# Two merge stages of a one-core hybrid layer: seven block products in place of eight, with sums by accumulating transfers and on VectorE

## The reference

```python
o_a = attend(q_a, k_all, v_all) @ w_pa
...
o_g = rms_norm(o_g, g_gla).reshape(B, T, GLA_V) * jax.nn.silu(r_g)
o_g = o_g @ w_pg
g_a, g_b = jnp.split(jax.nn.sigmoid(gates), 2, axis=-1)
mix = (g_a * o_a + g_b * o_g) @ w_out
```

## Time and profile before

| | us |
|---|---|
| median of 3 runs | 2679.12 (2678.48 to 2681.05) |
| the profiled execution | 2678.96 |
| its span | 2677.1 |
| TensorE busy | 2538.2 (95%) |
| VectorE busy | 1662.4 (62%) |
| ScalarE busy | 1329.9 (50%) |
| GpSimd busy | 285.5 (11%) |

### The profile page before, as it was taken

How to read it: one execution, slowest core, us unless ns; L and a number is a source line. 1 busy time by engine, 2 the same in 40 slices (tenths; PEclk the granted TensorE clock), 3 DMA queues, 4 the chain that set the end, 5 groups by cost and what they waited for, 6 DMA issues and landing times.

```text
span 2677.1 us, 37871 instructions
## 1 busy us (share of the span) xinstructions
PE 2538.2 (95%) x15199; PEld 1938.3 (72%) x15199; DVE 1662.4 (62%) x2553; ACT 1329.9 (50%) x2262; POOL 285.5 (11%) x287
## 2 busy tenths in 40 slices
PE   7999699999999999999999999996899999999994
PEld 3574499999788587676767888883677777777773
DVE  2654678886333435757576434656777767777775
ACT  3542467776423324444344332442666767666663
POOL 1441101000000001010101000000010101111012
PEclk9999899999999999999999999997899999999997
DMA  9320000000211100101012201535698888989886
GB/s 332 129 90 8 0 1 1 1 1 1 73 38 71 62 16 20 36 18 38 7 34 83 79 32 37 192 118 211 229 313 308 273 315 288 313 282 310 304 273 215
DMA packets 176608, 345.06 MB, mean 129 GB/s; under 512 B 9338, under 2 KB 37580, under 8 KB 176434
## 3 DMA queue, kind: packets, MB, share of 16 engines
q1 hardware_dynamic: 166396, 314.09, 32.9%
q0 software_dynamic: 9472, 28.32, 4.1%
q10 hardware_dynamic: 566, 0.24, 0.0%
HBM read 304.35 MB, written 38.27 MB: 128 GB/s over the span
## 4 chain that ended last, share of the span: by engine, by line
PE 63%; issue 22%; DMA 8%; DVE 4%; ACT 2%; POOL 1%; SPq 0%; POOLq 0%; DVEq 0%; ACTq 0%
PE ps L1100 16%; PE ps L1449 7%; PE ps L851 6%; DMA ffn_scratch<-WK 6%; PE ps L823 5%; PE ps L1409 5%; PE ps L228 4%; PE ps L1991 4%; PE ps L1512 2%; PE ps L1495 1%; PE ps L1423 1%; PE ps L2556 1%; PE ps L2017 1%; PE ps L1472 1%; PE ps L1393 1%
## 5 line engine op out<-in xcount | busy, mean ns | idle before, releaser
L2617 ACT ACTIVATE RWr<-R 128x1024 fp32r<-128x1024 f32 x384 | 377.8, 1054 | 73.6 <-PE ps L2556 69.9
L2712 DVE TENSOR_TENSOR W_low<-R,RWr 128x1024 fp32r<-128x1024 f32 x256 | 301.5, 1221 | 77.3 <-ACT RWr L2617 75.2
L2556 PE MATMUL ps<-RWr,R1r 128*128 128x512 f32 x1024 | 329.6, 396 | 6.0 <-DVE R1r L2700 4.2
L1100 PE MATMUL ps<-W_high,tile_high 128*128 128x512 f32 x640 | 250.9, 392 | 7.8 <-DVE W_low L1178 7.3
L1100 PE MATMUL ps<-W_low,tile_high 128*128 128x512 f32 x640 | 250.4, 391 | 0.0
L1100 PE MATMUL ps<-W_high,tile_low 128*128 128x512 f32 x640 | 250.4, 391 | 0.0
L2556 PEld LDWEIGHTS ps<-RWr,R1r 128*128 128x128 f32 x1024 | 193.0, 188 | 58.2 <-issue 14.2
L1170 DVE TENSOR_TENSOR tile_low<-R,tile_high 128x1024 fp32r<-128x1024 f32 x80 | 97.9, 1224 | 156.8 <-ACT tile_high L1126 156.6
L1449 PE MATMUL ps<-R3r 128*128 128x512 f32 (+1 forms) x640 | 188.5, 371 | 2.9 <-issue 2.9
L2712 DVE TENSOR_TENSOR tile_high<-R,RWr 128x1024 fp32r<-128x1024 f32 x128 | 150.9, 1220 | 29.9 <-ACT RWr L2617 29.6
L2556 PE MATMUL ps<-RWr,R3r 128*128 128x512 f32 x512 | 167.7, 399 | 0.0
(11 more groups left out here) (373 smaller groups left out, 5069.8 us busy)
## 6 DMA issues: line engine op xcount, KB each, us to landing
R<-in_w_dram SPq DMA_DIRECT2D x96, 2048.0 KB, 13.3
RW<-in_w_in_dram SPq DMA_DIRECT2D x11, 1024.0 KB, 5.3
R<-in_w_mod_dram SPq DMA_DIRECT2D x5, 2048.0 KB, 14.0
RW<-in_w_in_dram SPq DMA_DIRECT2D x5, 2048.0 KB, 7.8
RW<-in_w_mod_dram SPq DMA_DIRECT2D x4, 2048.0 KB, 12.1
WK<-in_w_mod_dram SPq DMA_DIRECT2D x3, 2048.0 KB, 7.7
mix_scratch<-R SPq DMA_DIRECT2D x10, 512.0 KB, 2.6
R<-mix_scratch SPq DMA_DIRECT2D x10, 512.0 KB, 6.1
```

The lines of the kernel that those rows point to most:

```text
L1100: i = pe.matmul(bank(m % 4), Tsplit[a][:, m % 2, k, :], Wsplit[b][:, k, :], start=(k == 0 and n == 0), stop=(k == KD - 1 and n == 2))
L2556: m = pe.matmul(bank(bank_of(e, i, j)), stat[a][:, k, :], w[b][:, k % 2, :], start=(k == 0 and z == 0), stop=(k == KD - 1 and z == 2))
L2617: act.activation(ring_high[n % RING], pair_raw[i][j][:, 2 * q:2 * q + 2, :], ACT.Copy).then_inc(S("weights_high"), 1)
L2712: dve.tensor_tensor(ring_low[n % RING], pair_raw[i][j][:, 2 * q:2 * q + 2, :], ring_high[n % RING].bitcast(F32), ALU.subtract).then_inc(S( ...
```

## The change

Each product of (1280 x 1024) by (1024 x 1024) is now cut into blocks and done with seven block products in place of eight. Tiles are taken in five pairs p (tiles 2p and 2p+1 are the two block rows), the inner dimension in two halves of four chunks, the weight matrix in four blocks of 512 rows by 512 columns. A step is now one combination c of seven for one pair: 4 chunks by 3 matmuls, 12 in all, and there are 7 x 5 x 2 = 70 steps in a merge (two halves g of 35 steps; g is one whole product). Merge A does o_a first (g = 0) and its gates second (g = 1); merge B does its gates first.

- Rows: three of the seven combinations take raw rows; the others take sums S1, S2, S4, S3, which DVE makes in place (`rows_sum`, L1342 to L1350), 4 per pair, 40 per merge, 512 columns each. In the second half of merge A they go into the output blocks, since h is still needed.
- Weights: blocks are summed in place by 1 MB accumulating transfers from SBUF to SBUF that POOL issues (L1404), 4 per half, 8 per merge, each behind the one before it. Seven combinations by 4 chunks are split per half: 56 chunks per merge where 32 were.
- Outputs: c = 0 goes to a bank, ACT copies it out (`move`), c = 1 accumulates on the same bank and gives block 11. The others are summed by DVE into the output blocks (`block_sum`, L1329 to L1333), 60 per merge; c = 5 accumulates on the bank of c = 4 after DVE has read that bank. Six banks in a ring.
- Gates and products: sigmoid on ACT after the last sum of a block, then the product on DVE (`product`, L1365), 20 per merge. In merge A the product follows one or two steps behind the sum.
- Tiles are split three steps ahead, into four half-size buffers.
- Merge A's mix is stored when its rows are done, for odd tiles after c = 6, the last combination. Merge B no longer loads it: POOL adds it from `mix_scratch` at the end by ten accumulating transfers of 512 KB (L1416), and the output stage's first two turns wait for them.
- PE also waits for `state_moved` before merge B.

```diff
+        def staggered(x, y):
+            return [(x, 0), (x, 1), (y, 0), (x, 2), (y, 1), (x, 3), (y, 2), (x, 4), (y, 3), (y, 4)]
+        ORDER = staggered(0, 1) + [(c, p) for p in range(PAIRS) for c in (2, 3)] + staggered(4, 5) + [(6, p) for p in range(PAIRS)]
+        W_BLOCK = {0: (0, 0), 1: (1, 0), 2: (0, 0), 3: (1, 1), 4: (1, 1), 5: (0, 1), 6: (1, 0)}
+        ROW_SUM_OF = {2: "S1", 3: "S4", 4: "S2", 5: "S3"}
+        W_SUM_OF = {2: 1, 5: 2, 4: 3, 6: 4}
+        AHEAD = 3
+        BANKS = 6
+            w_split_at[-1 if C < 1 else 0 if C < 2 else last_step[C - 2] + (3 if C == COMBOS else 0)].append(C)
...
-                        for n, (a, b) in enumerate(((high, high), (high, low), (low, high))):
-                            i = pe.matmul(bank(m % 4), Tsplit[a][:, m % 2, k, :], Wsplit[b][:, k, :], start=(k == 0 and n == 0), stop=(k == KD - 1 and n == 2))
+                    if c == 1:
+                        pe.wait_ge(S("gates_made"), made["move", g, p])
+                    elif c == 5:
+                        pe.wait_ge(S("tiles_merged"), merged["sum", g, p, "12", 4])
+                    elif q >= BANKS:
+                        bank_read(pe, q - BANKS)
...
+                        if name == "S2":
+                            i = dve.tensor_tensor(S2, a11, S1, ALU.subtract)
+                        elif name == "S4":
+                            i = dve.tensor_tensor(S4, a12, S2, ALU.subtract)
+                        else:
+                            i = dve.tensor_tensor(S2, a22, S2, ALU.subtract)
...
+                    for nth, (dst, src, c) in enumerate(((r11, r12, 0), (r12, r22, 0), (r22, r11, 3), (r21, r22, 1))):
+                        pool.wait_ge(S("weights_split"), split + HALF_K * (c + 1))
+                        weights_landed(pool, g, nth)
+                        pool.dma_start(dst, src, accum_op=ALU.add).then_inc(S("tiles_in2"), 16)
...
+                            pool.wait_ge(S("tiles_merged"), merged["product", 1, p, "12" if i == 0 else "21"])
+                            pool.dma_start(mix[:, t, :], mix_dram[t * P:(t + 1) * P, :], accum_op=ALU.add).then_inc(S(f"tiles_in{i}"), 16)
...
-            for t in range(NT):
-                if t in (0, KD):
-                    sp.wait_ge(S("tile_out") if t == 0 else S("gated_out_turned"), GH * NI if t == 0 else GH * NT)
-                sp.dma_start(mix[:, t, :], mix_dram[t * P:(t + 1) * P, :]).then_inc(S("R3_moved"), 16)
...
+                if t < 2:
+                    pe.wait_ge(S(f"tiles_in{t}"), 16 * (len(range(t, NT, 3)) + PAIRS))
```

More of the change, by code:

```diff
@@ new lines, in dve_after @@
+        def dve_after(tag, m):
+            ops = []
+            for back, when in ((2, {4: ("12",), 5: ("22",), 6: ("21",)}), (1, {1: ("11",)})):
+                if 0 <= m - back < MS and (tag, steps_m[m - back][0]) == (0, 1):
+                    g, c, p = steps_m[m - back]
+                    ops += [("product", g, p, b) for b in when.get(c, ())]
+            if m + AHEAD < MS and steps_m[m + AHEAD][1] == 4:
+                g, c, p = steps_m[m + AHEAD]
+                ops.append(("rows", g, p, "S3"))
+            if m < MS:
+                g, c, p = steps_m[m]
+                for b in {2: ("22",), 3: ("12",), 4: ("12",), 5: ("22", "21"), 6: ("21",)}.get(c, ()):
+                    ops.append(("sum", g, p, b, c))
+                    if (tag, g) == (1, 1) and c >= 4 and (b, c) != ("21", 5):
+                        ops.append(("product", g, p, b))
+                if c == 1 and (tag, g) == (1, 1):
+                    ops.append(("product", g, p, "11"))
+            if 0 <= m - 1 < MS and steps_m[m - 1][1] == 1:
+                g, c, p = steps_m[m - 1]
+                ops += [("rows", g, p, name) for name in ("S1", "S2", "S4")]
+            return ops
@@ new lines, in counted @@
+        def counted(tag, after, base):
+            table = {}
+            for m in range(MS + 2):
+                for op in after(tag, m):
+                    table[op] = base + len(table) + 1
+            return table
+        act_done, dve_done, bases = [], [], (0, 0)
+        for tag in range(2):
+            act_done.append(counted(tag, act_after, bases[0]))
+            dve_done.append(counted(tag, dve_after, bases[1]))
+            bases = (bases[0] + len(act_done[tag]), bases[1] + len(dve_done[tag]))
@@ new lines, in act_merge @@
+                for m in range(MS + 2):
+                    if m + AHEAD < MS:
+                        tile_high(m + AHEAD)
+                    for C in w_split_at.get(m, ()):
+                        weights_high(C)
+                    ops = act_after(tag, m)
+                    for name, *at in ops:
+                        if name == "gate" and at[2] != "11":
+                            gate(*at)
+                    if m < MS and steps_m[m][1] < 2:
+                        act.wait_ge(S("merge_tile_done"), m0 + m + 1)
+                    for name, *at in ops:
+                        if name == "move":
+                            move(*at)
+                        elif at[2] == "11":
+                            gate(*at)
@@ new lines, in dve_merge @@
+                tile_low(0)
+                for C in w_split_at[-1]:
+                    weights_low(C)
+                tile_low(1)
+                for m in range(MS + 2):
+                    if m in behind:
+                        behind[m](dve, ch)
+                    if m == 0:
+                        for n in range(2, AHEAD):
+                            tile_low(n)
+                    if m + AHEAD < MS:
+                        tile_low(m + AHEAD)
+                    for C in w_split_at.get(m, ()):
+                        weights_low(C)
+                    for name, *at in dve_after(tag, m):
+                        if name == "rows":
+                            rows_sum(*at)
+                        elif name == "sum":
+                            dve.wait_ge(S("merge_tile_done"), m0 + m + 1)
+                            block_sum(*at)
+                        else:
+                            if at[2] == "11" and tag == 1:
+                                dve.wait_ge(S("merge_tile_done"), m0 + m + 1)
+                            product(*at)
```

351 lines of the change are left out of this document (222 added, 129 removed).

## The result

The changed kernel takes **2631.93 us** (median of four runs, 2627.85 to 2633.42) against 2680.09 us of the kernel before on the same chip: a ratio of 0.982, 95% interval 0.980 to 0.983, or 48 us less. The forecast was 2630 us, within 2620 to 2652. Two more rounds of the same kernel on other occasions gave 2634.05 and 2635.20 us (ratios 0.982 and 0.983); single runs of it lie between 2626 and 2636 us.

The account below looks back on a forecast made before the run. The prediction took the merges to be bound by the number of matmuls. Merge A's terms sum to -24.3 us and merge B's to -24.5, together -48.8 from 2678.96 us: 2630 us, range 2620 to 2652.

Parts of the forecast that it names:

- 120 matmuls fewer, each merge: Both merges: 960 matmuls become 840, all on the path at 0.2267 us each, 27.2 us less per merge.
- waits for VectorE, each merge: TensorE stalls 2.3 us beside steps 53 to 64 of the second half, 0.2 us in the first: 2.5 us.
- half-clock beginning, against before: Start of each merge: matmuls at half clock after TensorE stood still, said to come back whatever is done later.
- end of merge A: Between merge A's last matmul and GLA's first: block sum, sigmoid and product follow one another, 1.4 us more.
- start of merge B: First steps of merge B: two half-size steps ready before VectorE finishes GLA's last tiles, gain 0.3 us.
- weight sums: POOL's 1 MB transfers in both merges: cost 0 at 11.5 us each, costing from 15.3 us on.
- end of merge B, to the second turn of mix: After merge B: the last addition of mix lands between hidden and 1.3 us late, taken as 0.5 us.
- the rival of 2650 us: Both merges: each of 140 step starts costs TensorE a hand-over of 0.14 us, 19.6 us; chance 0.10.
- no stall: Both merges: VectorE's lag never reaches TensorE, so stalls vanish, 2625 us or 2623 us; chance 0.15.
- VectorE bound: Stretches of c = 4 and 5 in both merges: VectorE's slower instructions bound them, 2643 us; chance 0.17.
- the 17 pairs: Steps 53 to 64: 17 of 53 VectorE instructions directly behind what they read, each 0.12 us more.
- the rival that ended slower: Weight sums land late, costing 12L - 201 us at L us per transfer, 2729 us at 25; chance 0.07 beyond break-even.

Follow-up runs that it names:

- e7: Changed kernel with the block sum first in c = 4 steps and 18 and 28 identity products ahead of merges A and B: 2629.58 us, ratio 0.9815.
- e1: Changed kernel with VectorE's block sum put ahead of tile split and weight chunks in c = 4 steps: 2631.66 us, ratio 0.9815.
- e2: Changed kernel with twelve more VectorE subtractions of 512 columns in each merge's second half, beside steps 53 to 64: 2646.6 us, ratio 0.9875.
- e6: Changed kernel with 18 and 28 unused identity products on TensorE ahead of merges A and B: 2632.75 us, ratio 0.982.
- e8: Changed kernel with the block sum first in c = 4 steps and 8 and 11 identity products ahead of merges A and B: 2627.0 us, ratio 0.9795.
- after_third: The changed kernel with no edit, profiled a third time: 2635.2 us, ratio 0.983 to the kernel before.
- e3: Changed kernel with each 1 MB weight sum done as four chained transfers of 256 KB: 2631.23 us, ratio 0.983.
- e4: Changed kernel with each 1 MB weight sum done as eight chained transfers of 128 KB: 2730.3 us, ratio 1.019.
- e5: Changed kernel with the output stage's first turn of mix waiting for even and odd tiles' additions, not even only: 2644.17 us, ratio 0.987.

## Why the prediction was right

Term by term, in us of the forecast and of the traces:

| Term | forecast | measured |
|---|---|---|
| 120 matmuls fewer, each merge | -27.2 | -27.2 by count and pitch |
| start of merge A | -1.0 | -0.96 |
| waits for VectorE, each merge | +2.5 | +2.4 |
| half-clock beginning, against before | 0 | +0.4 and 0 |
| rest of merge A, not followed | 0 | +0.2 |
| end of merge A | +1.4 | +1.3 |
| start of merge B | -0.3 | -0.7 (gaps within its first five steps) |
| weight sums | 0 | 0 |
| end of merge B, to the second turn of mix | +0.5 | -0.1 |
| both merges | -48.8 | -49.5 |

**The count.** The pitch stayed at 0.2267 us in the long pieces (76.44 / 336 = 0.2275, in which the last matmul counts with its whole row), and 28 steps of 12 follow one another in a piece. A step's start costs TensorE nothing: the rival of 2650 us is out, and e7 shows it at its sharpest, 190.3 us for 840 matmuls.

**The waits.** They came where the prediction put them (the end of the stretch of c = 4 and 5) and for the instruction named, a block sum. The total is right to 0.1 us, 2.4 against 2.5, but that is luck in part. The term was made of 2.3 us in the second half and 0.2 in the first; 1.6 and 0.8 us were measured (0.37 and 1.04, 0.37 and 0.30 us of gaps, and 0.08 us behind each), two misses that cancel. The load of the stretch was counted nearly right: the 53 instructions are 53, and they take 35.8 us where 34.9 was said. But the prediction turned the whole excess over the matmuls' time into a wait, and e1 shows that this holds only for the order of the changed kernel: with the same instructions, taking 36.5 us, the wait is gone. The order inside the stretch, which the sum had no term for, decides. In that order little is absorbed: of e2's 7.2 us more, 5.3 to 5.8 us reach TensorE. The pitches were those of the earlier trace rows; VectorE's timeline of the changed kernel, three row sums of which each reads the one before:

```profile
687.44 0.68 DVE L1342 TENSOR_TENSOR R<-R 128x512 f32<-128x512 f32 x1
688.15 0.69 DVE L1346 TENSOR_TENSOR R<-R 128x512 f32<-128x512 f32 x1
688.88 0.69 DVE L1348 TENSOR_TENSOR R<-R 128x512 f32<-128x512 f32 x1
```

Their starts lie 0.71 and 0.73 us apart; 852.93 to 853.53, a sum and a tile part, is 0.60 us. The rule of the Trainium skill that I weighed before ("VectorE: DVE Perf Modes", "The DRAIN you can't avoid": a semaphore between VectorE instructions costs nothing extra, as measured with copies) does not hold for such pairs. The rival *no stall* falls with the four gaps, the rival *VectorE bound* with VectorE's 79% and with e1. That the 0.12 us of the 17 pairs made up the waits, as the sum had it, no run shows.

**The clock.** The half-clock beginning stayed, as said. I had left it out of the difference; it became slightly longer in merge A (12 slow matmuls against 10, though the stop before it is 1 us shorter; why is not shown) and nearly the same in merge B (9 against 8). "That comes back whatever is done later" was too strong: e6 and e8 show for merge A that it goes when the stop before it is filled, and in after_third merge B began without it.

**The sums.** My assumption of 11.5 us for 1 MB was too high. GpSimd's transfers on the page (count, KB each, median us from issue to landing):

```profile
RW<-RW POOLq DMA_DIRECT2D x16, 1024.0 KB, 7.0
```

The term was 0 all the same, since the worked-out limit was 15.3 us; e3 confirms no cost at 14.6 us and e4 the cost beyond (85 us where 89 was said), so the rival that ended slower was a real one and its condition was not met. Its chance rested on a row of scattered rows into DRAM, which did not bear on SBUF into SBUF.

**The ends.** Merge A's end is right to 0.1 us; the chain shows the three instructions that I counted (block sum, sigmoid, product; the counterpart of the earlier trace rows):

```profile
870.40 0.70 DVE R L1333
871.12 0.64 ACT R L1267
871.78 0.69 DVE R L1365
872.62 6.65 PE ps L1588 x46
```

Merge B's end cost nothing, and that was close. I had 6 to 11.5 us to landing and 10.2 us of cover (11.7 us less the 1.5 us until the issue). The cover is some 9.9 us (1633.44 - 1623.55) and the landing 9.5 to 10.1 us in the three profiles, so it came out between hidden by 0.4 us and 0.2 us late. A shorter merge or more beside the transfer brings it into the open, as e1, e7 and e8 show (1.0 to 2.1 us). In e5 I expected 5 to 7 us from the median landing, and more than 10 came: the last addition is among the slowest of the ten, and the median of all says little about it.

**What stays open.** From the second turn of mix to the end the changed kernel is 2.0 to 2.2 us longer than the kernel before in its three profiles. By the prediction a change of more than 2 us behind the merges was a sign of being wrong, and this stands at that line. e2 (995.2), e8 (996.5) and e7 (997.4) have less with the same code there, so it need not belong to the change, but there is only one profile of the kernel before (996.2) to set against it. Open too are why one start of merge B ran at full clock after the same stop, why the last addition lands later in e1, e7 and e8, and the 2.3 us in e8's GLA stage.

## What to carry to other kernels

When work is taken from the engine that is always busy and given to a second one, look for the stretch in which the second one's own work piles up, and put the instruction for which the first waits ahead of the bulk work: here the order cost 2.5 us per merge, and the same work in the other order nothing. Work out for every new transfer the time at which it would begin to cost, not only its likely duration, and take its duration from rows with the same neighbours on the DMA engines (5.2 us at the shortest, 9.5 to 12.0 us beside loads). Before a gain is counted, look at what hid behind the time that goes: with the merge shorter by e1's order, a transfer behind it came into the open and took 1.9 of the 5 us back. Where the busy engine waits some us for its first operands, products without use that just fill the wait kept its clock in merge A; too many of them gave the gain back. In merge B one unfilled start, in after_third, kept it too, so a gain is best read against several profiles of the unedited kernel.

## What the runs showed of the hardware

- A sum of 1 MB from SBUF into SBUF by an accumulating transfer lands 7.0 us after its issue; 256 KB take 3.3 us (median of 64, e3) and 128 KB 2.7 us (median of 128, e4). The issue keeps GpSimd for about 0.9 us. A transfer of an eighth of the size takes over a third of the time.
- The same accumulating transfer of 512 KB from DRAM took between 5.2 and 9.6 us in the changed kernel and up to 12.0 us in e1; the last of the ten, issued within 0.5 us of two loads of 512 KB, is among the longest each time.
- TensorE's granted clock fell to the lower level after a stop of 4.7 us within a merge that had run at the upper one for over 170 us (e2), but not at the stops of 1.04 us in the changed kernel and 1.96 us in e2. At the start of merge B an idle time of 3.44 us was followed by the lower level in e5 and not in after_third.
- An fp32 product of 128 x 128 with 128 columns runs as two instructions of about 0.12 us each (16 in 2.05 us, e8).
- On VectorE two neighbours of 512 columns start 0.60 us apart where they are independent, 0.71 to 0.73 us where the second reads what the first wrote, and 0.80 us (852.13 to 852.93) from a gate product to a block sum that waits for it by semaphore and reads PSUM.
